# A gated-recurrence decoder layer on one core: three chunks of keys turned through scratch memory in one set of transfers, squares and broadcast moved apart

## The reference, cut to what matters

```
h    = rms_norm(x, norm_g) * (1 + scale) + shift
qa, ka, va, za, qb, fb, ib, zb = split(h @ w_in)
ya   = window_attention(qa, ka, va) * silu(za)
f    = lb + (1 - lb) * sigmoid(fb);   k = (1 - lb) * sigmoid(-fb)
# per chunk of tokens, per head:  L = cumsum(log f)
o    = (q * exp(L)) @ S + A(q, k, decay) @ v
S    = exp(L_end) * S + (k * exp(L_end - L)).T @ v
yb   = rms_norm(o, o_norm_g) * silu(zb)
y    = g_a * (ya @ w_proj_a) + g_b * (yb @ w_proj_b)
out  = x + gate * (y @ w_out)
```

## Time and profile before

| | us |
|---|---|
| three runs | 1553.02, 1554.44, 1556.95 (median 1554.44) |
| the profiled execution's own time | 1554.78 |
| its span, first to last instruction | 1552.7 |
| TensorE busy | 1516.0 (98%) |
| VectorE / ScalarE / GpSimd busy | 803.8 / 535.0 / 831.5 |
| granted TensorE clock, mean | 0.996 |

### The profile page before, as it was taken

One profiled execution on the slowest core, in us unless ns is written; L12 is line 12 of the kernel. 1 busy time (PEld: TensorE's weight loads), 2 busy tenths in 40 slices (PEclk: granted clock), 3 DMA queues, 4 the chain that ended last, 5 costly groups with the idle time before them and its releaser, 6 DMA issues.

```text
span 1552.7 us, 31555 instructions
## 1 busy us (share of the span) xinstructions
PE 1516.0 (98%) x12936; PEld 1233.5 (79%) x12936; DVE 803.8 (52%) x1972; ACT 535.0 (34%) x1111; POOL 831.5 (54%) x1074
## 2 busy tenths in 40 slices
PE   5999999999999999999999999999999999999998
PEld 2777778777888777888779878888788977788886
DVE  5767466225558856422444774642253775642122
ACT  4334322434312531344331452243432352243330
POOL 1525433567863643367683472447696363436671
PEclk9999999999999999999999999999999999999999
DMA  9612212534563321443343231244544231244351
GB/s 346 236 55 83 83 57 82 171 117 165 172 202 110 104 69 57 129 143 136 110 164 136 90 122 43 87 120 148 190 165 147 76 110 56 70 123 123 108 169 58
DMA packets 119047, 191.52 MB, mean 123 GB/s; under 512 B 57198, under 2 KB 74951, under 8 KB 118120
## 3 DMA queue, kind: packets, MB, share of 16 engines
q1 hardware_dynamic: 118904, 189.52, 37.0%
HBM read 169.13 MB, written 18.25 MB: 121 GB/s over the span
## 4 chain that ended last, share of the span: by engine, by line
PE 92%; DVE 5%; issue 1%; ACT 1%; DMA 0%; SPq 0%; DVEq 0%
PE ps_D L801 54%; PE ps_D L798 25%; PE ps_XCD L863 1%; PE ps_XB L939 1%; PE ps_XA L964 1%; PE ps_XA L975 1%; PE ps_XA L1001 1%; PE ps_XB L992 1%; PE ps_XB L991 1%; PE ps_XA L939 1%; PE ps_XB L975 1%; DMA s_st_lo<-in_x_prompt 0%; DVE sm L1254 0%; PE ps_XCD L964 0%; DVE sm L1257 0%
## 5 line engine op out<-in xcount | busy, mean ns | idle before, releaser
L1757 POOL TENSOR_TENSOR w_lo_t<-w_raw,w_hi_t 128x256 fp32r<-128x256 f32 x920 | 687.2, 780 | 582.4 <-ACT w_hi_t L1023 582.1
L801 PE MATMUL ps_D<-h_hi_t,w_hi_t 128*128 128x512 f32 x1024 | 409.1, 399 | 0.0
L801 PE MATMUL ps_D<-h_lo_t,w_hi_t 128*128 128x512 f32 x1024 | 399.4, 390 | 0.0
L801 PE MATMUL ps_D<-h_hi_t,w_lo_t 128*128 128x512 f32 x1024 | 399.3, 390 | 0.0
L1023 ACT ACTIVATE w_hi_t<-w_raw 128x1024 fp32r<-128x1024 f32 x232 | 239.9, 1051 | 112.9 <-PE ps_D L798 61.0
L801 PEld LDWEIGHTS ps_D<-h_hi_t,w_hi_t 128*128 128x128 f32 x1024 | 192.2, 188 | 48.0 <-issue 10.0
L801 PEld LDWEIGHTS ps_D<-h_hi_t,w_lo_t 128*128 128x128 f32 x1024 | 192.2, 188 | 41.3
L801 PEld LDWEIGHTS ps_D<-h_lo_t,w_hi_t 128*128 128x128 f32 x1024 | 192.5, 188 | 37.0
L798 PE MATMUL ps_D<-w_hi_t,h_hi_t 128*128 128x384 f32 (+1 forms) x384 | 141.7, 369 | 1.1 <-DVE yf_t L1391 1.0
L798 PE MATMUL ps_D<-w_lo_t,h_hi_t 128*128 128x384 f32 (+1 forms) x384 | 136.7, 356 | 0.0
L798 PE MATMUL ps_D<-w_hi_t,h_lo_t 128*128 128x384 f32 (+1 forms) x384 | 136.4, 355 | 0.0
(11 more groups left out here) (389 smaller groups left out, 2323.1 us busy)
## 6 DMA issues: line engine op xcount, KB each, us to landing
w_raw<-in_w_blocks SPq DMA_DIRECT2D x232, 512.0 KB, 3.4
xr<-in_x_prompt SPq DMA_DIRECT2D x16, 512.0 KB, 5.2
x_or_AT<-in_x_prompt SPq DMA_DIRECT2D x14, 512.0 KB, 5.4
out_dram<-xr SPq DMA_DIRECT2D x12, 512.0 KB, 2.9
z_o<-kk SPq DMA_DIRECT2D x8, 512.0 KB, 3.1
x_or_AT<-in_x_turned SPq DMA_DIRECT2D x3, 1024.0 KB, 6.0
p_or_hf<-in_x_turned SPq DMA_DIRECT2D x3, 1024.0 KB, 5.6
z_k<-kk SPq DMA_DIRECT2D x4, 512.0 KB, 4.7
```

The source lines that it names most:

```text
L801: ins = mm(bank[:, :], w[:, s0, k0 + k, :], a[:, k, :], start=go, stop=end)
L1757: ins = g_.tensor_tensor(w_lo[:, c, k:k + 2], w_raw[:, n % NRAW, k:k + 2], f32(w_hi[:, c, k:k + 2]), ALU.subtract)
```

## The change

Chunk 1's keys are turned the way chunks 2 and 3 were: `kD` turns three chunks in one DVE instruction (1536 instead of 1024 elements on each partition), one DMA writes them to `z_k` (768 KB in runs of 1536 bytes), four DMAs of 192 KB read them back. `KT` is left for chunk 0 alone. `st` of chunks 1, 2 and 3 waits for all four reads, and ACT's `o` of chunks 1 to 3 waits for the write. The two events stand at 27 instead of 28. The squares of tiles 2 and 3 stand one unit earlier (41 and 42), so does the reload of the x tiles on SP (43 instead of 44), and `bc` stands behind unit 53 half 0 instead of unit 52 half 1.

```diff
@@ -130,9 +130,8 @@
 
-KEYS_TURNED = (1,)
 O_AT, ON_AT, YD_AT, YT_AT = (57, 59, 61, 63), (60, 64), (65, 66, 69, 70), (66, 67, 70, 71)
-KS_AT, KL_AT, OS_AT, OL_AT = (28, 28), (28, 28), (30, 32), (31, 32)
+OS_AT, OL_AT = (30, 32), (31, 32)
 
...
@@ -198,12 +197,11 @@
     for _t in range(NT):
-        if _t // 2 not in KEYS_TURNED:
-            put(it, 28 + _t, 0, "KT", _t, "XC")
+        if _t == 0:
+            put(it, 28, 0, "KT", 0, "XC")
         at_half(it, O_AT[_t], "o", _t, "XB")
         at_half(it, O_AT[_t], "st", _t, "XA")
-    for _r in KEYS_TURNED:
-        at_half(it, 56, "kD", _r)
+    at_half(it, 56, "kD", 0)
     for _r in range(2):
...
@@ -211,9 +209,9 @@
         for _n, _t in enumerate((2, 3, 0, 1)):
-            put(it, (42, 43, 46, 47)[_n], 1, "xst", _t)
+            put(it, (41, 42, 46, 47)[_n], 1, "xst", _t)
         put(it, 50, 1, "rstd", 0)
-        put(it, 52, 1, "bc", 0, "XA")
+        put(it, 53, 0, "bc", 0, "XA")
         for _n in range(4):
...
@@ -413,7 +411,7 @@
         first.close()
-        k_turned = first.enter_context(nc.sbuf_tensor("k_turned", [P, 2, HB, 2, P], F32))
+        k_turned = first.enter_context(nc.sbuf_tensor("k_turned", [P, HB, 3, P], F32))
         first.close()
...
@@ -426,7 +424,8 @@
                     for t in (acc_kst[:, :], qq.rearrange("p h n -> p (h n)")[:, 0:1024])]
-        zk, zo = (nc.dram_tensor(f"z_{n}", [2, 4, 32, 2 * HB, 4, 32], F32).ap() for n in "ko")
+        zk = nc.dram_tensor("z_k", [4, 32, 3 * HB, 4, 32], F32).ap()
+        zo = nc.dram_tensor("z_o", [2, 4, 32, 2 * HB, 4, 32], F32).ap()
         y_hi, y_lo = sb("y_hi_t", [P, KT, TB], F32R), sb("y_lo_t", [P, KT, TB], F32R)
...
@@ -558,14 +557,14 @@
                     later.setdefault(b0 + 33, []).append(("xst", it, 0))
-                    later.setdefault(b0 + 44, []).append(("x01", it, 0))
+                    later.setdefault(b0 + 43, []).append(("x01", it, 0))
                     later.setdefault(b0 + 48, []).append(("xh", it, 0))
                     later.setdefault(b0 + (50 if it else 59), []).append(("xh", it, 1))
                 later.setdefault(b0 + 5, []).append(("vr", it, 0))
                 for r in range(2):
-                    if r in KEYS_TURNED:
-                        later.setdefault(b0 + KS_AT[r], []).append(("ks", it, r))
-                        later.setdefault(b0 + KL_AT[r], []).append(("kl", it, r))
+                    if r == 0:
+                        later.setdefault(b0 + 27, []).append(("ks", it, 0))
+                        later.setdefault(b0 + 27, []).append(("kl", it, 0))
                     later.setdefault(b0 + OS_AT[r], []).append(("os", it, r))
...
@@ -586,14 +585,14 @@
                 if what == "ks":
-                    s.wait_ge("kD", len(KEYS_TURNED) * it + KEYS_TURNED.index(a) + 1)
-                    s.wait_ge(f"kt_in{a}", 64 * it)
-                    load(zk[a].rearrange("i q (h t) j p -> (i q) h (t j p)", t=2), kk[:, :, half], f"kz{a}")
+                    s.wait_ge("kD", it + 1)
+                    s.wait_ge("kt_in", 64 * it)
+                    load(zk.rearrange("i q (h t) j p -> (i q) h (t j p)", t=3), kk[:, :, P:TB], "kz")
                 elif what == "kl":
-                    s.wait_ge(f"kz{a}", 16 * (it + 1))
+                    s.wait_ge("kz", 16 * (it + 1))
                     for j in range(4):
-                        load(k_turned[32 * j:32 * j + 32, a].rearrange("p h t (i c) -> p (h t) i c", c=32),
-                             zk[a, :, :, :, j].rearrange("i q n p -> q n i p"), f"kt_in{a}")
+                        load(k_turned[32 * j:32 * j + 32].rearrange("p h t (i c) -> p (h t) i c", c=32),
+                             zk[:, :, :, j].rearrange("i q n p -> q n i p"), "kt_in")
                 elif what == "os":
...
@@ -992,12 +991,12 @@
                 elif task == "st":
-                    if a < 2:
+                    if a == 0:
                         s.freed(it, "KT", a)
                     else:
-                        s.wait_ge("kt_in1", 64 * (it + 1))
+                        s.wait_ge("kt_in", 64 * (it + 1))
                     for h in range(HB):
-                        left = kst[:, h, :] if a < 2 else k_turned[:, 1, h, a % 2, :]
+                        left = k_turned[:, h, a - 1, :] if a else kst[:, h, :]
                         ins = mm(bank[:, P * h:P * h + P], left, ibtok[:, a, P * h:P * h + P],
...
@@ -1169,15 +1168,13 @@
                     s.full(*key)
-                    if a:
-                        s.full(it, "st", a - 1)
                     s.free(fn(kst, bank[:, :].rearrange("p (h n) -> p h n", h=HB), ACT.Copy), *key)
                 elif task == "o":
                     s.full(*key)
                     if it or a:
                         s.freed(*((it, "o", a - 1) if a else (it - 1, "o", 3)))
-                    if a // 2 in KEYS_TURNED:
-                        s.wait_ge(f"kz{a // 2}", 16 * (it + 1))
+                    if a:
+                        s.wait_ge("kz", 16 * (it + 1))
                     s.wait_ge("yl", 16 * it + 4)
...
@@ -1595,8 +1592,7 @@
                 elif task == "kD":
-                    half = kk[:, :, 256 * a:256 * a + 256]
-                    do(v.transpose(half, half), "kD")
+                    do(v.transpose(kk[:, :, P:TB], kk[:, :, P:TB]), "kD")
                 elif task == "onorm":
                     s.freed(it, "o", 2 * a + 1)
                     c, half = slice(8 * a, 8 * a + 8), kk[:, :, 256 * a:256 * a + 256]
```

More of the change, by code:

```diff
@@ L267 @@
         + [f"w_in{n}" for n in range(NRAW)] + ["w_hi", "w_lo", "burst", "th_full", "kk", "sq", "ssq", "qa", "k_sc",
-           "lvl", "dgp", "at0", "smax", "p_exp", "p_norm", "kst", "kD", "kz0", "kz1", "kt_in0", "kt_in1", "oD", "oz0", "oz1", "ot_in0", "ot_in1", "yt", "yf", "yh", "yl", "y7f", "y7h", "y7l", "x_in0", "x_in1", "xst", "rstd",
+           "lvl", "dgp", "at0", "smax", "p_exp", "p_norm", "kst", "kD", "kz", "kt_in", "oD", "oz0", "oz1", "ot_in0", "ot_in1", "yt", "yf", "yh", "yl", "y7f", "y7h", "y7l", "x_in0", "x_in1", "xst", "rstd",
            "xn", "xm", "xh0", "xh1", "h_hi", "h_lo", "grow", "s_rows", "s_th", "s_sq8", "s_sc", "s_exp", "s_p", "ckv", "s_oT",
```

## The result

The changed kernel took 1568.51 us (median of 6 runs, 1563.82 to 1570.01) against 1554.49 for the kernel before (6 runs, 1552.58 to 1558.33): a ratio of 1.0081, 95% interval [1.0070, 1.0092]. The forecast was 1563.3 with a range of 1557.8 to 1567.0: right in its sign and in the place of the loss, 5 us too low. The profiled execution took 1567.67 us over a span of 1565.5, 12.8 more than the span of before. The medians differ by 14.0: this execution lies 0.8 under the changed kernel's median, and the one of before 0.3 over its own.

A forecast was written before the change was run, and what follows sets the result against it. The prediction took TensorE, fed almost without a gap, as the bound; 6.7 + 2.3 - 1.8 + 0.3 + 1.4 = 8.9 us slower gave 1563.7 us for the profiled execution, 1563.3 as median, range 1557.8 to 1567.0.

The forecast's parts named there:

- The step on the wait: Iteration 0, burst at unit 29: TensorE waits for block 29's load, queued behind write and reads; 6.7 us, bounds 5.2 to 7.9.
- The step on the clock: Iteration 0, behind the burst's wait: TensorE runs at half clock for a while; 2.3 us more, between 0 and 3.
- The step on the broadcast: Moved broadcast, iterations 1 and 2: TensorE waits for bank D1, then still does the broadcast; 0.7 us slower each, 1.4 us.
- The transposes: Chunk 1's four transposes leave TensorE in each of four iterations; 0.44 us each, 1.8 us less.
- The reads late for the state: Chunk 1's `st`, iterations 1 to 3: reads nearly in time, 0.3 us added; as rival 1.2 us late each, chance 0.12.
- The squares and the reload of x: Squares at unit 41, x reload at 43: moving them earlier costs nothing; if cover failed, some 0.6 us three times.
- The DVE turn: `kD` on DVE takes 0.6 us longer, hidden by DVE's 5.1 us idle behind it; it makes the transfers begin later.

The follow-up runs named there:

- a_order: The changed kernel with the write and its four reads one unit later in SP's queue (28) in iteration 0 only; 1558.68 us, ratio 1.0023.
- d_only27: The kernel before with the write and its four reads one unit earlier in SP's queue (27) in all iterations; 1564.34 us, ratio 1.0055.
- c_fill64: The changed kernel with 64 extra, overwritten matmuls ahead of the burst that waits in iteration 0; 1558.91 us, ratio 1.0023.
- f_order_bc: a_order with the broadcast back at unit 52's second half; 1553.56 us, ratio to the kernel before 1.0000.
- b_bcback: The changed kernel with only the broadcast put back to unit 52's second half; 1564.45 us, ratio 1.0060.
- h_rstd_before: The kernel before with only rstd issued two units earlier on VectorE; 1550.08 us, ratio 0.9975.
- g_best: f_order_bc with rstd issued two units earlier on VectorE; 1551.02 us, ratio to the kernel before 0.9978.
- p_after24: The changed kernel with 24 more matmuls of 64 columns ahead of block 29's burst in iteration 0; 1562.93 us, ratio 1.0043.
- e_onlybc: The kernel before with only the broadcast moved half a unit later; 1557.99 us, ratio 1.0028.
- p_before48: The kernel before with 48 more matmuls of 64 columns ahead of block 29's burst in iteration 0; 1557.71 us, ratio 1.0018.

## Why the prediction was wrong

**The place and the mechanism in iteration 0 held.** SP's order made the burst wait for block 29, and a_order and d_only27 show that this is the bulk of the loss.

**The step on the wait: 6.7 us forecast, 7.7 measured**, inside its bounds. The failed sentence is "Four reads keep SP busy 2.8 us". They took 4.16, and SP issues the load behind all of them. Most of the growth is the size: at the old place four reads took 2.8 us at 128 KB and 4.1 at 192 (a_order). Some of it is the place: in d_only27, at 128 KB, they took 3.33. I let the size grow the landing by 1.2 us and the issue by nothing; from the first read's issue to the burst it was 9.2 us, where I had taken 8.0 and 8.4 was my larger figure. The burst came 4.97 us after the load's issue, against the 4.4 of the earlier trace rows.

**The step on the clock: 2.3 forecast, 3.2 measured**, over its bound of 3. The mechanism was right (c_fill64). I took less than the row gave by allowing for luck that the row didn't show.

**The step on the broadcast: 1.4 forecast, 2.7 measured.** The waits were 0.6 us longer each, as forecast with 0.7 (the argument on bank D1 was right). What failed is that it priced a longer wait only by its length: at 1.9 to 2.2 us the wait reaches where the clock may fall, which costs 1.5 us more each time that it does, once in this trace. I had the waits of up to 1.6 us as harmless and that of 2.6 as not the earlier trace rows, had 0.7 on top of 1.6 in my own sum, 2.3 us, and never asked on which side it falls.

**The transposes: -1.8 forecast, -2.0 in the trace. The reads late for the state: +0.3 forecast, nothing in the changed kernel**, as no line of its waits names `k_turned`. **The squares and the reload of x**: no run moves them alone. f_order_bc keeps them moved, and beside its own kernel before it is 1.8 us over what was expected, which its trace puts at the gap near 783, so a cost is neither shown nor excluded. The DVE turn made the transfers begin later, as said, and cost nothing else.

**Not in the sum at all: 2.0 us of gaps**, 1.7 where TensorE waits for its instructions and 0.3 where it waits for GpSimd. The former did not follow the change: the gap at 4881 was 1.53 us in the changed kernel, 1.26 in a_order, 1.01 in b_bcback and 1.03 in f_order_bc, all with the same instructions around it; 0.95 in the kernel before, 1.34 in h_rstd_before. How long it is depends on when the block's transfer began and how long it took: 1.1 us after TensorE had entered the block ahead, and 0.93 us, in the changed kernel; 0.5 and 0.93 in the kernel before; 0.6 and 1.44 in g_best, with a gap of 1.54. The wait for GpSimd was 0.65 to 2.37 us over the 18 traces. I count these 2 us as spread between executions, not as an effect of the change; with one trace of each kernel that is argued, not shown.

**The range** ended at 1567.0. Its upper end for the forecast put every term at a bound, but it stopped short of a clock drop at the broadcast, for which it had no term. Two drops there, as in the traces of a_order and p_after24, are possible too: the two slowest executions of the changed kernel had a mean granted clock of 0.991 against 0.993 in the profiled one, which would fit a second drop but doesn't show where it was. Put together, the terms that were too small add 1.0 + 0.9 + 1.3 + 2.0 us, those too large and a start 0.6 us shorter take 1.1 off: 8.9 + 4.1 = 13.0.

## What to carry to other kernels

Before moving a blocking event up in a shared DMA queue, list every load that now stands behind it and when each is needed: one unit sooner cost 9 us here (0.0081 less 0.0023), and with the kernel before's smaller transfer it still cost 8.5. Price a wait on TensorE by its length and by whether it takes the clock down; two waits of 1.3 and 1.6 us are cheaper than two of 1.9 and 2.2 by far more than the 1.2 us between them. To remove a wait for a short chain, start the chain sooner rather than its reader later: two units on VectorE's idle time won 0.25%, half a unit on TensorE lost 0.28%.

## What the runs showed of the hardware

- **Waits near 2 us sometimes drop the clock.** One of 1.90 us did in a_order and did not in the changed kernel; one of 2.17 did there and of 2.18 in a_order, 2.18 did not in e_onlybc, nor 2.29 in h_rstd_before. Behind the start of the program, those of 4.4 us and more all did, and none of up to 1.7 us. Windows of a_order, where the waits ended at 754.12 and 1123.52:

```profile
754.00:756.00 2.00, 1.88 (x6) 0.81 0.03 8
756.00:758.00 2.00, 2.00 (x18) 0.50 0.00 0
...
1123.00:1126.00 3.00, 2.48 (x7) 0.65 0.41 167
```

- **It fell without any idleness** in p_before48, among matmuls of 64 columns.
- **DMA issue grows with the size**: over the four iterations of all 18 traces, four reads in runs of 128 bytes took SP 2.8 to 3.6 us at 128 KB each, 3.7 to 4.6 at 192 KB each.
- **TensorE can wait for its own instructions.** In runs of small matmuls it stood up to 1.7 us at the border of a block of 256 instructions, and went on 1.2 to 1.6 us after the block's 16 KB had landed. Where the borders fall decides how long it stands: 24 useless matmuls ahead won 0.20% in the kernel before and 0.35% behind g_best, net of their own time.
